# Reordering the attention heads of a two-layer block, with the neighbour mask on GpSimd

## The reference

```
a_out = neighbourhood_attention(...)          # scores + relative bias, window mask
b_out = diff_attention(dq[0], dq[1], dk[0], dk[1], v, lam, slopes)   # softmax1 @ v - lam * softmax2 @ v
b_out = rms_norm(b_out, diff_subln[l]) * (1.0 - lambda_init)         # per head of 64
c_out = gqa_attention(cq, ck, v)              # grouped queries, norm and rope ahead
d_out = mla_attention(q_nope, q_rope, k_nope, k_rope, v)
mix = concatenate([a_out, b_out, c_out, d_out]) @ w_o[l]
x = x + rms_norm(mix, post_mix_norm[l])
h = rms_norm(x, pre_ffn_norm[l]);  x = x + rms_norm(swiglu(h), post_ffn_norm[l])
```

## Time and profile before

| | |
|---|---|
| median of 3 runs | 1952.02 us (1951.75 to 1952.05) |
| the profiled execution | 1952.05 us |
| its span | 1950.3 us |
| TensorE busy | 1883.0 us (97%) |
| VectorE, ScalarE, GpSimd busy | 1341.6, 995.9, 70.9 us |
| mean granted TensorE clock | 0.99 |

### The profile page before, as it was taken

How to read it: one execution, slowest core, us unless ns; L and a number is a source line. 1 busy time by engine, 2 the same in 40 slices (tenths; PEclk the granted TensorE clock), 3 DMA queues, 4 the chain that set the end, 5 groups by cost and what they waited for, 6 DMA issues and landing times.

```text
span 1950.3 us, 34519 instructions
## 1 busy us (share of the span) xinstructions
PE 1883.0 (97%) x13470; PEld 1730.4 (89%) x13470; DVE 1341.6 (69%) x2141; ACT 995.9 (51%) x1534; POOL 70.9 (4%) x82
## 2 busy tenths in 40 slices
PE   8999999999999999999999999998999999999998
PEld 8978999897899987899989789998989998979997
DVE  5757888675788876788877578885555555665555
ACT  7755333765633376633374453346655334655333
POOL 3002000000000000000000000002400000000000
PEclk9999999999999999999999999999999999999999
DMA  8527988532788842588843368884435554324552
GB/s 286 194 87 233 358 310 309 190 135 87 276 324 308 310 158 98 209 322 315 310 176 146 116 236 325 309 307 174 148 112 194 184 193 159 122 87 178 188 194 86
DMA packets 60355, 412.22 MB, mean 211 GB/s; under 512 B 8592, under 2 KB 8784, under 8 KB 11616
## 3 DMA queue, kind: packets, MB, share of 16 engines
q1 hardware_dynamic: 55728, 401.33, 55.7%
q0 software_dynamic: 4528, 9.56, 1.8%
HBM read 409.71 MB, written 3.16 MB: 212 GB/s over the span
## 4 chain that ended last, share of the span: by engine, by line
PE 81%; DVE 10%; ACT 4%; DVEq 2%; issue 2%; ACTq 1%; DMA 0%; SPq 0%
PE psu L501 33%; PE psy L660 16%; PE psy L563 6%; PE psy L609 5%; PE psy L555 4%; PE psu L518 3%; PE psm L735 3%; DVE wlo L854 3%; PE psu L720 2%; PE psy L631 2%; PE psy L542 1%; PE pso L706 1%; DVE ada_raw L1016 1%; DVE x L1083 1%; ACT whi L845 1%
## 5 line engine op out<-in xcount | busy, mean ns | idle before, releaser
L845 ACT CAST whi<-raw 128x2048 fp32r<-128x2048 f32 (+1 forms) x281 | 536.0, 1908 | 625.1 <-PE psu L501 424.5
L854 DVE TENSOR_TENSOR wlo<-raw,whi 128x2048 fp32r<-128x2048 f32 (+5 forms) x296 | 644.2, 2177 | 276.3 <-ACT whi L845 275.3
L501 PE MATMUL psu<-hhi,whi 128*128 128x256 f32 x1920 | 537.0, 280 | 0.0
L501 PE MATMUL psu<-hlo,whi 128*128 128x256 f32 x1920 | 536.0, 279 | 0.0
L501 PE MATMUL psu<-hhi,wlo 128*128 128x256 f32 x1920 | 535.8, 279 | 0.0
L501 PEld LDWEIGHTS psu<-hhi,whi 128*128 128x128 f32 x1920 | 360.8, 188 | 3.0
L501 PEld LDWEIGHTS psu<-hlo,whi 128*128 128x128 f32 x1920 | 360.8, 188 | 2.4
L501 PEld LDWEIGHTS psu<-hhi,wlo 128*128 128x128 f32 x1920 | 360.8, 188 | 0.0
L1016 DVE CUSTOM_DVE_ANT_0 ada_raw<-ada_raw,cvec 128x1024 f32<-128x1024 f32 x192 | 226.9, 1219 | 1.4 <-DMA ada_raw<-ada 1.4
L660 PE MATMUL psy<-whi,ahi 128*128 128x512 f32 x528 | 210.5, 399 | 1.0 <-DVE alo L1035 0.9
L660 PE MATMUL psy<-wlo,ahi 128*128 128x512 f32 x528 | 208.0, 394 | 0.0
(11 more groups left out here) (342 smaller groups left out, 3035.0 us busy)
## 6 DMA issues: line engine op xcount, KB each, us to landing
raw<-wts SPq DMA_DIRECT2D x280, 1024.0 KB, 4.8
ada_raw<-ada SPq DMA_DIRECT2D x96, 1024.0 KB, 4.9
dense_bias<-rel_bias POOLq DMA_DIRECT2D x32, 64.0 KB, 12.3
nab<-dense_bias SPq DMA_DIRECT2D x2, 1024.0 KB, 7.4
ada_raw<-fox_rows POOLq DMA_DIRECT2D x4, 512.0 KB, 7.1
cb<-cst POOLq DMA_DIRECT2D x1, 1408.0 KB, 8.6
cb<-cst SPq DMA_DIRECT2D x1, 1056.0 KB, 10.4
x<-x_in SPq DMA_DIRECT2D x2, 512.0 KB, 4.6
```

Of the source, the lines that this page charges most:

```text
L501: last = mm(psu[:, bank, cc * SEQ:(cc + 1) * SEQ], a[:, cols], h[:, kt, :], start=(kt == 0 and j == 0), stop=(kt == KT - 1 and j == 2))
L845: nc.scalar.copy(whi[:, part_of(c), 0:n], raw[:, slot_of(c), 0:n]).then_inc(hi_done, 1)
L854: last = nc.vector.tensor_tensor(wlo[:, part_of(c), cols], raw[:, slot_of(c), cols], whi[:, part_of(c), cols].bitcast(f32), ALU.subtract)
```

## The change

The items are taken in another order: grouped-query 0 to 3, differential 4 to 11, neighbourhood 12 to 15, latent 16 to 19. With it the first two turns, now of the grouped-query heads, move from slots 24 and 25 to 17 and 19, the turns 2 and 3 are those of the differential heads, and the sums, the root and the scaling move to slots 26 and 27. The columns of the output rows and the rows of `w_o` follow. The transposes of the grouped queries use another PSUM bank. The neighbour mask is added by GpSimd in one instruction over the whole table, with its own semaphore. In the fox layer GpSimd's adds with a broadcast operand become adds of a per-partition scalar, one per head.

```
-           [24, 25, 28, 29, 30, 31, 33, 35], "00 01 10 02 03 11 12 13",
+           [17, 19, 28, 29, 30, 31, 33, 35], "00 01 10 02 03 11 12 13",
...
+                pool.wait_ge(na_loaded, 16 * (l + 1))
+                pool.wait_ge(cb1_loaded, 16)
+                nb = fold(nab[:], 32, 64)
+                mask = cb[:, CB1["na"][0]:CB1["na"][1]]
+                nc.gpsimd.tensor_tensor(nb, nb, mask.unsqueeze(1).to_broadcast([P, 32, 64]), ALU.add).then_inc(na_ready, 1)
                 pool.wait_ge(x_ready, 8 + 8 * l)
...
-                nc.gpsimd.tensor_tensor(first, rows4[:, :, 0:P], own, ALU.add)
-                nc.gpsimd.tensor_tensor(rows4[:, :, P:], rows4[:, :, P:], later, ALU.add).then_inc(fox_sum, 1)
-                pool.wait_ge(fox_sum, g4 + 1)
-                nc.gpsimd.tensor_tensor(rows4[:, :, 0:P], rows4[:, :, 0:P], later, ALU.add)
+                for i in range(4):
+                    h = 4 * g4 + i
+                    nc.gpsimd.tensor_scalar(first[:, i], rows4[:, i, 0:P], lcq[:, h:h + 1], None, ALU.add)
+                nc.gpsimd.drain()
+                for i in range(4):
+                    h = 4 * g4 + i
+                    nc.gpsimd.tensor_scalar(rows4[:, i], rows4[:, i], lcq[:, 16 + h:17 + h], None, ALU.add)
+                nc.gpsimd.drain()
...
-                if m < 2:
+                if m in (2, 3):
                     pe.wait_ge(mix_ready, l + 1)
                 else:
-                    pe.wait_ge(o_evac, I0 + 2 * m + 6)
+                    pe.wait_ge(o_evac, I0 + (2 * m + 2 if m < 2 else 2 * m + 6))
...
-                                512 + h * HD, table=na_table(h),
+                                512 + h * HD, table=na_table(h), tpre=(na_ready, l + 1),
...
-            return out[4:12] + out[0:4] + out[12:]
+            return out
...
-                            nc.tensor.transpose(psu[:, 1, k * SEQ + t * P:k * SEQ + (t + 1) * P],
+                            nc.tensor.transpose(psy[:, 2, k * SEQ + t * P:k * SEQ + (t + 1) * P],
...
-                if h == 22:
+                if h == 27:
                     act.wait_ge(sub_sum, l + 1)
...
-                if h == 19:
-                    neighbour_mask(0, 1)
-                if h == 21:
-                    neighbour_mask(1, 1)
-                if h == 22:
+                if h == 26:
                     sub_sums()
-                    neighbour_mask(2, 2)
-                if h == 23:
+                if h == 27:
                     sub_norm()
...
-        w_o = a["w_o"][l].reshape(4, 256, D)[[1, 2, 0, 3]]
-        w_o[1] = w_o[1].reshape(4, HD, D)[[0, 2, 1, 3]].reshape(256, D)
+        w_o = a["w_o"][l].reshape(4, 256, D)[[2, 1, 0, 3]]
+        w_o[0] = w_o[0].reshape(4, HD, D)[[0, 2, 1, 3]].reshape(256, D)
```

More of the change, by code:

```diff
@@ L243, in build @@
         na_loaded = sem("na_loaded")
+        na_ready = sem("na_ready")
         silu_done = sem("silu_done")
@@ L283, in build @@
         fox_tab = sem("fox_tab")
-        fox_sum = sem("fox_sum")
         g_logit = sem("g_logit")
@@ L476, in _ @@
                 first = fold(nab[:, g4 * 512:(g4 + 1) * 512], 4, P)
-                own, later = (lcq[:, at + 4 * g4:at + 4 * g4 + 4].unsqueeze(2).to_broadcast([P, 4, P]) for at in (0, 16))
-                nc.gpsimd.tensor_tensor(first, rows4[:, :, 0:P], own, ALU.add)
-                nc.gpsimd.tensor_tensor(rows4[:, :, P:], rows4[:, :, P:], later, ALU.add).then_inc(fox_sum, 1)
-                pool.wait_ge(fox_sum, g4 + 1)
-                nc.gpsimd.tensor_tensor(rows4[:, :, 0:P], rows4[:, :, 0:P], later, ALU.add)
+                for i in range(4):
[6 more added lines that the diff above has]
+                nc.gpsimd.drain()
                 nc.gpsimd.tensor_tensor(first, first, mask, ALU.add)
@@ L1117, in heads1 @@
                                     [gv[:, kc * P + kv * HD:kc * P + (kv + 1) * HD] for kc in range(2)],
-                                    256 + (2 * c + kv) * HD, pre=(gqa_ready, l + 1), vpre=(bank_free, b0 + 4)))
+                                    (2 * c + kv) * HD, pre=(gqa_ready, l + 1), vpre=(bank_free, b0 + 4)))
             for h in range(4):
@@ L1124, in heads1 @@
                                     [dfv[:, kc * 256 + h * HD:kc * 256 + (h + 1) * HD] for kc in range(2)],
-                                    h * HD, table=distance_table, slope=2.0 ** (-8.0 * (h + 1) / 4), pair=which,
+                                    256 + h * HD, table=distance_table, slope=2.0 ** (-8.0 * (h + 1) / 4), pair=which,
                                     pre=(bank_free, b0 + 6), vpre=(bank_free, b0 + 7)))
@@ L1280, in act_mix1 @@
                     act.wait_ge(gq_tr, l + 1)
-                    nc.scalar.activation(gqT, psu[:, 1], ACT.Copy, scale=HD ** -0.5)
+                    nc.scalar.activation(gqT, psy[:, 2], ACT.Copy, scale=HD ** -0.5)
                     nc.scalar.copy(gkT, psy[:, 3, 0:SEQ]).then_inc(gqa_ready, 1)
@@ L1371, in latent_rope @@
                                       kr.unsqueeze(2).to_broadcast([P, NT, 4, 32])).then_inc(ml_rope, 1)
-            dh = rows[:, :, 0:256]
+            dh = rows[:, :, 256:512]
             dh4 = dh.rearrange("p t (h d) -> p t h d", h=4)
@@ L1391, in sub_norm @@
                                         ALU.mult).then_inc(mix_ready, 1)
-            def neighbour_mask(h0, n):
-                dve.wait_ge(na_loaded, 16 * (l + 1))
-                for h in range(h0, h0 + n):
-                    bias = fold(nab[:], NT, 4, 4, 64)[:, :, h]
-                    mask = cb[:, CB1["na"][0]:CB1["na"][1]].unsqueeze(1).unsqueeze(1).to_broadcast([P, NT, 4, 64])
-                    nc.vector.tensor_tensor(bias, bias, mask, ALU.add)
             for h in range(MIX.slots):
```

## The result

The changed kernel takes 1964.7 us (median of 6 runs, 1963.45 to 1968.62), against 1951.88 us of the kernel before beside it (6 runs, 1949.0 to 1953.84). The ratio is 1.0073, with a 95% interval of 1.0059 to 1.0086; it is close to the quotient of the two means (1965.46 and 1951.37, 1.0072), where the quotient of the medians is 1.0066. By the medians it is slower by 12.8 us; the forecast was 1953.3 us, and the time lies above the range of 1945.5 to 1960.5. The profiled execution took 1967.35 us around a span of 1965.6 us, 15.3 more than that of before.

What follows compares the result with a forecast made beforehand. TensorE, busy nearly all of the span, was taken as the bound. Added 0.6 + 5.4 + 9.4 = 15.4 us against 14.2 removed made it 1.2 us slower: 1953.3 us, called no change, range 1945.5 to 1960.5.

Steps and rivals of the forecast that it cites:

- The fox layer: Fox layer: GpSimd's eight scalar adds and two drains per group cost nothing; bounds 0 and 1 us.
- sign of being wrong: Fox layer: its stretch moving by more than 1 us would show the prediction wrong.
- Case B: Layer 0: GpSimd's mask add also blocks a VectorE multiply-reduce; 3.5 us idle plus 1.7 clock, 1958.5 us; chance 0.25.
- Removed: Slots 22 to 25, both layers: the old stall and its half clock go, 14.2 us in all.
- Slot 12: Layer 0: the first scores wait 0.6 us for ScalarE's copy of gkT; bounds 0 and 1.
- The GpSimd add: Neighbour mask: the one 128x2048 add on GpSimd takes about 5.0 us; bounds 4.1 and 5.2.
- The block in layer 1: Slot 14: GpSimd's add holds VectorE's split; 2.9 us idle before slot 16's score plus 2.5 clock, 5.4 us.
- The rule of the Trainium skill: Shared SBUF port: the first engine keeps it for its whole instruction, so the 2.9 us would be had in full.
- Slot 28: Both layers: the turn waits 3.0 us for VectorE's scalings, plus 1.7 of clock; 4.7 us per layer.
- C: GpSimd and VectorE: no block of any length, so 5.4 us less, 1947.8 us; chance 0.20.
- D: TensorE: the idle comes but the clock stays up in most places, 4.7 us faster, 1947.3 us; chance 0.12.
- such falls as its own spread: Every clock fall, also at later norm boundaries, may be one stretch or two; the forecast's own range is 1950 to 1957.

Runs made afterwards that it cites:

- e1: The changed kernel with the fox layer's GpSimd adds of before, three wide adds and one semaphore per group: 1959.03 us.
- e6: The changed kernel with its scalar adds kept and the fox layer's GpSimd drains replaced by semaphore waits: 1957.94 us.
- e10: The changed kernel with fox adds of before, mask on VectorE in slots 19, 20, 21, 23, and slot 26's split in 27 ahead of the scalings: 1941.09 us.
- e3: The changed kernel with the neighbour mask back on VectorE in slots 19, 21 and 22: 1954.88 us.
- e11: e10 with the four turns of slots 28 to 31 one slot later: 1950.36 us.
- e12: e11 with the mask on GpSimd in eight adds of 128x256 instead of on VectorE: 1951.78 us.
- e4: The changed kernel with the GpSimd mask add cut into eight of 128x256: 1956.2 us.
- e8: The changed kernel with GpSimd awaiting all four fox rows before its first scalar add, drains kept: 1970.8 us (one run).
- e2: The kernel before with the fox layer's part of the change alone: 1959.54 us.
- e5: The changed kernel with the weight split of slot 26 moved to slot 27, behind the scalings: 1963.78 us.

## Why the prediction was wrong

**The step that failed** is "The fox layer. ... so nothing; the bounds are 0 and 1 us". It priced the eight adds and took the drains for free. The first drain lasted until GpSimd's own loads in flight had landed, and this cost 5.9 us in the stretch (5.7 by the median of e1, 6.8 by that of e6). The prediction's own sign of being wrong, that the fox layer's stretch moves by more than 1 us, came. The step also looked at the second group's table, with 9 us to spare, and not at the first. In the trace of before that one was ready at 1359.9 us and first read at 1364.17:

```profile
1358.59 1.29 POOL L483 TENSOR_TENSOR ada_raw<-ada_raw,cb 128x512 f32<-128x512 f32 x1
```

```profile
1364.17 0.28 DVE L815 CUSTOM_DVE_ANT_0 work<-psu,nab 128x128 f32<-128x128 f32 x1
```

It had 4.3 us to spare. The first group went from 6.8 us to 17.6: 6.56 of drain, and 10.9 of adds (4.45 + 3.88 + 1.30 + 1.27). That uses up the 4.3 and leaves VectorE 5.6 us late, counted from the start of the stretch.

The price of the adds looks right and is so by luck. Undisturbed they take 4 x 0.6 + 3.63 + 1.30 + 1.27 = 8.6 us, for 8.5. But the 6.7 us from which the prediction set out are not undisturbed: they hold a first add of 2.14 us beside a split of VectorE, and without it the old group takes 3 x 1.04 + 2 x 1.29 = 5.7. With every add of scalars as dear per element as the slowest add (1.29 us for 512 columns), the new group would take 3.9 + 2.6 = 6.5, not 8.5. An add of scalars is dearer per element than any of the old ones.

**Case B came**, with a chance of 0.25 in the prediction. It said 3.5 us of idle and 1.7 of clock; the trace has 2.69 and 3.4, 6.1 in place of 5.2. What it named as open is now shown: the multiply-reduce with two SBUF tensors is held as a split is. The step priced "against: it is not shown that this instruction is blocked" too high. Case B alone would have given 1958.5 us, the fox layer alone 1953.3 + 5.9 = 1959.2; either is inside the range, and both together are not. Their sum is 1964.4, against 1964.7 measured. That it fits to 0.3 us is in part luck: the profiled execution is 2.65 us above the median, and 2.5 us of its difference lie outside the places of the sum.

**Right, with sizes.** Removed: 14.2 us, measured 21.05 - 13.97 + 20.84 - 13.99 = 13.9. In e10, where only the first wait, 2 x 0.87 and 2 x 0.16 stand against it, the two layers are shorter by 5.1 + 5.9 = 11.0, where 14.2 - 0.6 - 1.7 - 0.3 = 11.6 was due. Slot 12: 0.6, measured 0.60. The GpSimd add: 5.0, measured 4.73 and 4.55. The block in layer 1: 2.9 idle and 2.5 clock, measured 2.26 and 3.4, 5.7 for 5.4. The rule of the Trainium skill that the prediction weighed, "SBUF — State Buffer", section "Who interferes with whom" (whichever of the two engines is first keeps the shared port for the whole of its instruction), agrees with these traces. The blocked instruction ended 1.09 us behind the end of the other in layer 0 (79.28 against 78.19) and 2.16 us in layer 1, which is about what it takes alone, 1.21 and 2.29. Slot 28: 3.0 and 1.7 per layer, measured 2.54 and 1.7. Layer 1 as a whole was to be 5.4 + 4.7 - 7.0 = 3.1 longer and is 2.9; layer 0, with the 6.1 us measured for B, 0.6 + 4.7 - 7.2 + 6.1 = 4.2, is 4.0.

**Rivals C and D fell** for this kernel: in its trace both blocks are of full length, and each of the four idle times of 2.3 to 2.7 us in question had a fall behind it. For D that is no rule. The 2.54 us of slot 28 in layer 0 of e3 and the 2.63 of slot 18 in layer 0 of e6 had none (granted clock 1.00 over the 11 us behind each), and two idle times of 1.6 and 1.5 us had one in three of four layers of e11 and e12. The 0.87 of e10 and the 0.44 of e4 had none. What decides it between 1.5 and 2.7 us no run here shows.

**Not in the sum:** 1.3 us between the mixing of layer 1 and the next norm, where a stretch at half clock is 6.83 us (503.13 to 509.96, granted clock 0.50) in place of 3.41 (497.93 to 501.35). The prediction named such falls as its own spread. The same place shows 3.41 us in e8, which has the changed kernel's code there, and 6.83 in e2, which has that of before, so the change is not its cause. The last 1.2 us of the profiled executions' difference lie in the rest of the program, 0.6 of them behind the fox layer, and were not traced further.

## What to carry to other kernels

Look for what a synchronising instruction waits on beside the work ahead of it: here a drain of GpSimd, which issues its own loads, was a wait for these loads, and a semaphore on the last writer was not. Where one engine can hold another for a whole instruction, cut the long instruction, even at a cost on the engine that has time, or keep it where it was: e4 came within 1.3 us of e3. A stall in an in-order chain is removed by putting the long step where its own engine waits for somebody else; later or earlier by one slot may only hand the stall to the next in the queue.

## What the runs showed of the hardware, not expected

- GpSimd's first drain, begun with loads of its own in flight: 5.10 to 9.62 us to the next instruction, which came 0.61 to 0.63 us behind the landing of the last load in all five traces; with none in flight 1.09 us; later ones 0.15 to 0.17.
- A waiting engine gets in between two instructions of the other that follow each other with only a read of 0.08 us between them: GpSimd asked at 73.46 us, inside the first multiply-reduce, and the second found it at work. In e4 VectorE's split came in between two of eight GpSimd adds.
- GpSimd's add of a scalar per partition: four of 128x256 take 3.63 us undisturbed, 0.92 each, against 1.04 us for one add of two tensors of 128x512, so per element it is nearly twice as dear.
- Between the changed kernel and e5, a difference of 0.7 us between the landing of a load and an instruction of another engine decides 6.1 us (2.69 idle and 3.4 of clock).
